# Recurrence heads of a hybrid decoder block: queries and keys scaled up the levels, the next head's projections in eight pieces

## What is computed

```python
qf = jax.nn.silu(q)
log_f = jnp.logaddexp(jnp.log(lb), jnp.log1p(-lb) + jax.nn.log_sigmoid(z))
k = -jnp.expm1(log_f)
def step(state, inp):            # one chunk of 64 tokens
    q_, k_, lf, v_ = inp
    b = jnp.cumsum(lf, axis=2)
    diff = b[:, :, :, None, :] - b[:, :, None, :, :]
    decay = jnp.exp(jnp.where(causal, diff, -jnp.inf))
    scores = jnp.einsum('bhtk,bhsk,bhtsk->bhts', q_, k_, decay)
    o = (jnp.einsum('bhts,bhsv->bhtv', scores, v_)
         + jnp.einsum('bhtk,bhkv->bhtv', q_ * jnp.exp(b), state))
    new_state = (jnp.exp(b_last)[..., None] * state
                 + jnp.einsum('bhsk,bhsv->bhkv', k_ * jnp.exp(b_last[:, :, None, :] - b), v_))
```

## Time and profile before

| | |
|---|---|
| runs (3) | 1618.0 to 1621.55 us, median 1621.48 us |
| profiled execution | 1621.46 us; span of its instructions 1619.6 us |
| PE, share of the span | 90% busy |
| VectorE, ScalarE | 50%, 40% busy |
| this stage | 155.6 to 362.6 us of the span |

### The profile page before, as it was taken

The page is one execution under the profiler, slowest core; times in us unless marked ns, Lnnn a source line. Parts: engine busy times, 40 slices in busy tenths (PEclk is TensorE's granted clock), DMA queues, the critical chain, the costliest instruction groups (busy, mean ns, idle before and its releaser), DMA issues. The chain is left out here.

```text
span 1619.6 us, 19494 instructions
## 1 busy us (share of the span) xinstructions
PE 1464.4 (90%) x7862; PEld 1222.1 (75%) x7862; DVE 805.5 (50%) x971; ACT 644.6 (40%) x760; POOL 108.0 (7%) x86
## 2 busy tenths in 40 slices
PE   6999789869886899979999999999699999995997
PEld 5887667757665688858888888988588888884786
DVE  5410677763332553421222113415489999885654
ACT  5310455421111432211111113133288888885554
POOL 0000000000000000000000000012312222221000
PEclk9999799979999899989999999999599999997999
DMA  6201100004212111122122113721689999994231
GB/s 222 79 1 39 33 14 14 26 4 115 53 26 51 28 41 51 39 61 59 58 69 61 58 58 124 254 92 53 264 322 380 389 385 389 383 370 182 79 110 46
DMA packets 103767, 205.66 MB, mean 127 GB/s; under 512 B 12944, under 2 KB 72976, under 8 KB 90128
## 3 DMA queue, kind: packets, MB, share of 16 engines
q1 hardware_dynamic: 94480, 187.88, 33.1%
q0 software_dynamic: 9216, 16.80, 2.8%
HBM read 188.38 MB, written 28.84 MB: 134 GB/s over the span
## 5 line engine op out<-in xcount | busy, mean ns | idle before, releaser
L1248 DVE TENSOR_TENSOR two_chunk_lo<-two_chunk_raw,two_hi 128x2048 fp32r<-128x2048 f32 x96 | 217.2, 2287 | 21.0 <-ACT two_hi L1244 20.8
L1244 ACT CAST two_hi<-two_chunk_raw 128x2048 fp32r<-128x2048 f32 x96 | 181.2, 1918 | 7.1 <-DMA two_chunk_raw<-w_e 7.1
L220 DVE TENSOR_TENSOR mix_w_lo<-mix_w_raw,mix_w_hi 128x1024 fp32r<-128x1024 f32 (+1 forms) x58 | 67.6, 1170 | 215.3 <-ACT mix_w_hi L216 215.3
L173 PE MATMUL two_banks<-mix_hT_hi,mix_w_hi 128*128 128x512 f32 x256 | 100.5, 393 | 10.0 <-DVE mix_w_lo L220 10.0
L2241 PE MATMUL two_banks<-two_hi,two_xT_hi 128*128 128x512 f32 x256 | 104.0, 406 | 4.2 <-DVE two_xT_lo L1584 4.2
L216 ACT CAST mix_w_hi<-mix_w_raw 128x1024 fp32r<-128x1024 f32 (+1 forms) x58 | 56.9, 986 | 111.6 <-PE two_banks L175 93.2
L2243 PE MATMUL two_banks<-two_hi,two_xT_lo 128*128 128x512 f32 x256 | 101.3, 396 | 0.0
L2242 PE MATMUL two_banks<-two_chunk_lo,two_xT_hi 128*128 128x512 f32 x256 | 101.3, 396 | 0.0
L174 PE MATMUL two_banks<-mix_hT_lo,mix_w_hi 128*128 128x512 f32 x256 | 100.3, 392 | 0.0
L175 PE MATMUL two_banks<-mix_hT_hi,mix_w_lo 128*128 128x512 f32 x256 | 100.3, 392 | 0.0
L173 PE MATMUL gate_gates<-mix_hT_hi,mix_w_hi 128*128 128x512 f32 x192 | 76.5, 398 | 4.5 <-DVE mix_w_lo L220 4.5
(11 more groups left out here) (288 smaller groups left out, 3360.2 us busy)
## 6 DMA issues: line engine op xcount, KB each, us to landing
two_chunk_raw<-w_e SPq DMA_DIRECT2D x102, 1024.0 KB
mix_w_raw<-w_in SPq DMA_DIRECT2D x44, 512.0 KB, 3.8
two_r<-results SPq DMA_DIRECT2D x16, 512.0 KB, 5.0
vals_w_raw<-w_in SPq DMA_DIRECT2D x12, 512.0 KB, 8.6
heads_values<-x SPq DMA_DIRECT2D x8, 512.0 KB, 11.5
reten_swapped<-reten_raw SPq DMA_DIRECT2D x8, 512.0 KB, 5.3
mix_w_raw<-w_b SPq DMA_DIRECT2D x8, 512.0 KB, 4.8
two_x<-x SPq DMA_DIRECT2D x8, 512.0 KB, 6.5
```

The lines of the kernel that those rows point to most:

```text
L173: nc.tensor.matmul(out, sh, mh, start=(k == 0), stop=False)
L220: self.nc.vector.tensor_tensor(self.lo[:, u, 0:kt], self.raw[:, u, 0:kt], self.hi[:, u, 0:kt].bitcast(F32), ALU.subtract).then_inc(self.lo ...
L1244: self.nc.scalar.copy(self.high(n)[:], self.raw(n)[:]).then_inc(self.hi_ok, 1)
L1248: self.nc.vector.tensor_tensor(self.low(n)[:], self.raw(n)[:], self.high(n)[:].bitcast(F32), ALU.subtract).then_inc(self.lo_ok, 1)
```

## The change

The logarithm, the running sum and the exponentials go. ScalarE makes f, the forget gate, and k times its gain directly. `block_totals` multiplies f pairwise up the levels, so that for every block of 1, 2, 4, ... 64 tokens the product of f over it is there. Q starts as q times f and K as k; after the pair of a level, `scale` multiplies, in place, the keys of each lower block by the total of the upper one and the queries of each upper block by the total of the lower one. The levels go from h = 1 up to h = 32. Behind the last, Q and K are what the state terms need, so the former `q_in` and `k_out` go too. Values are read from `values` directly; the GpSimd copy goes. The next head's two projections are cut into eight pieces of 12 matmuls each and put between the pairs; turned keys have two banks of their own, state products use the pair banks and these, and results go into the z sums' banks. Loops over heads are written out.

```diff
+    PAIRED, UP = NL + 1, 2 * NL
+    PIECES = [(half, part) for half in range(2) for part in range(2)]
...
-        ga, gb_, gc = m.sb("sig_z", [P, S]), m.sb("sig_minus_z", [P, S]), m.sb("sig_q", [P, S])
-        q, k, b = m.sb("q", [P, S]), m.sb("k", [P, S]), m.sb("b", [P, S])
-        X = m.sb("scaled", [P, 3, S])
-        q_in, k_out = m.sb("q_in", [P, S]), m.sb("k_out", [P, S])
+        f, q = m.sb("f", [P, S]), m.sb("q", [P, S])
+        Q, K, totals = m.sb("q_scaled", [P, 2, S]), m.sb("k_scaled", [P, 2, S]), m.sb("totals", [P, 2, S])
...
-        kv = m.ps("kv", [P, 4, P])
-        outs = m.ps("outs", [P, 4, HG_DV])
+        turned = [m.ps("turned0", [P, 4, P]), m.ps("turned1", [P, 4, P])]
...
+        kv = [[pairs[:, n].rearrange("p t c -> p (t c)").rearrange("p (t v) -> p t v", v=P) for n in range(2)],
+              [turned[0], turned[1]]]
...
+        def outs(half):
+            return sums[:, 1, half].rearrange("p (t v) -> p t v", v=P)
...
+        def total(i, h):
+            start = S - 2 * S // h
+            return f[:] if h == 1 else totals[:, i % 2, start:start + S // h]
...
-        @block.gpsimd
-        def _(pool):
-            def head(i):
-                if not first(i):
-                    pool.wait_ge(out_ok, 2 * i)
-                nc.gpsimd.tensor_copy(v[:], values[:, :, bass.ds(i * HG_DV, HG_DV)]).then_inc(v_ok, 1)
-            over(pool, HG_HEADS, head)
...
-            def level(i, l):
-                act.wait_ge(sub, 2 * NL * i + 2 * l + 2)
-                nc.scalar.activation(X[:, l % 3, :], X[:, l % 3, :], ACT.Exp).then_inc(expd, 1)
...
+            def gates_z(i):
                 act.wait_ge(projected, 2 * i + 1)
+                nc.scalar.activation(sig_z[:], z_of(i), ACT.Sigmoid).then_inc(sig, 1)
+                nc.scalar.activation(sig_minus_z[:], z_of(i), ACT.Sigmoid, scale=-1.0).then_inc(sig, 1)
+                act.wait_ge(sig, 3 * i + 1)
+                if i:
+                    act.wait_ge(up, UP * (i - 1) + 2)
+                nc.scalar.activation(f[:], sig_z[:], ACT.Identity, bias=lb[:, 1, i:i + 1],
+                                     scale=lb[:, 2, i:i + 1]).then_inc(f_ok, 1)
+                act.wait_ge(sig, 3 * i + 2)
+                nc.scalar.activation(K[:, i % 2], sig_minus_z[:], ACT.Copy, scale=lb[:, 2, i:i + 1]).then_inc(k_ok, 1)
+            def gates_q(i):
                 act.wait_ge(projected, 2 * i + 2)
+                if i:
+                    act.wait_ge(q_ok, i)
+                nc.scalar.activation(sig_q[:], sums[:, 0].rearrange("p a b -> p (a b)"), ACT.Sigmoid).then_inc(sig, 1)
+            gates_z(0)
+            ring.split_hi(act, 1, 0)
+            gates_q(0)
+            ring.split_hi(act, 1, 1)
+            for i in range(HG_HEADS):
+                if i + 1 < HG_HEADS:
+                    gates_z(i + 1)
+                if i + 2 < HG_HEADS:
+                    ring.split_hi(act, i + 2, 0)
+                for half in range(2):
                     act.wait_ge(k_turned, 2 * i + half + 1)
+                    nc.scalar.copy(k_tok[:, 4 * half:4 * half + 4, :], turned[half][:]).then_inc(k_tok_ok, 1)
+                if i + 1 < HG_HEADS:
+                    gates_q(i + 1)
+                if i + 2 < HG_HEADS:
+                    ring.split_hi(act, i + 2, 1)
                 for half in range(2):
                     act.wait_ge(out_ok, 2 * i + half + 1)
+                    nc.scalar.copy(values[:, 4 * half:4 * half + 4, i * HG_DV:(i + 1) * HG_DV],
+                                   outs(half)).then_inc(out_stored, 1)
...
-            def exponents(l):
-                h = LEVELS[l]
-                lower, upper = halves(b[:], h)
-                x_lower, x_upper = halves(X[:, l % 3, :], h)
-                ref = lower[:, :, h - 1:h].to_broadcast([P, S // (2 * h), h])
-                nc.vector.tensor_tensor(x_upper, upper, ref, ALU.subtract).then_inc(sub, 1)
-                nc.vector.tensor_tensor(x_lower, ref, lower, ALU.subtract).then_inc(sub, 1)
...
+            def block_totals(i):
+                dve.wait_ge(f_ok, i + 1)
+                for n in range(NL):
+                    h = 1 << n
+                    if n:
+                        dve.wait_ge(total_ok, NL * i + n)
+                    even, odd = even_odd(total(i, h))
+                    nc.vector.tensor_tensor(total(i, 2 * h), even, odd, ALU.mult).then_inc(total_ok, 1)
+            def queries(i):
+                dve.wait_ge(sig, 3 * i + 3)
+                nc.vector.tensor_tensor(q[:], sums[:, 0].rearrange("p a b -> p (a b)"), sig_q[:], ALU.mult).then_inc(q_ok, 1)
+                dve.wait_ge(q_ok, i + 1)
+                dve.wait_ge(f_ok, i + 1)
+                nc.vector.tensor_tensor(Q[:, i % 2], q[:], f[:], ALU.mult).then_inc(q_scaled, 1)
+            def scale(i, n):
+                h = 1 << (n - 1)
+                of_lower, of_upper = even_odd(total(i, h))
+                dve.wait_ge(paired, PAIRED * i + n + 1)
+                if n == 1:
+                    dve.wait_ge(q_scaled, i + 1)
+                else:
+                    dve.wait_ge(total_ok, NL * i + n - 1)
+                    dve.wait_ge(up, UP * i + 2 * n - 2)
+                lower = halves(K[:, i % 2], h)[0]
+                nc.vector.tensor_tensor(lower, lower, bc(of_upper, 2, h), ALU.mult).then_inc(up, 1)
+                upper = halves(Q[:, i % 2], h)[1]
+                nc.vector.tensor_tensor(upper, upper, bc(of_lower, 2, h), ALU.mult).then_inc(up, 1)
+            def mask(i, n):
+                level = NL - n
+                dve.wait_ge(paired, PAIRED * i + n + 1)
+                if i or n:
+                    dve.wait_ge(masked, PAIRED * i + n)
+                if i and n == 0:
+                    dve.wait_ge(out_ok, 2 * i)
+                nc.vector.tensor_copy(tick[:, level:level + 1], lb[:, 3, 0:1]).then_inc(ticked, 1)
+                nc.vector.copy_predicated(scores[:], bc(masks[:, level, :], 1, TT), pairs[:, n % 2]).then_inc(masked, 1)
+            def states(i, g):
+                dve.wait_ge(kv_ok, 2 * i + g + 1)
+                if g == 0:
+                    dve.wait_ge(total_ok, NL * i + NL)
+                if i and g == 0:
                     dve.wait_ge(out_ok, 2 * i)
                     dve.wait_ge(state_ok, SU * i)
+                for c in range(8 * g, min(8 * g + 8, SU)):
+                    if c:
+                        dve.wait_ge(state_ok, SU * i + c)
+                    nc.vector.scalar_tensor_tensor(out=state[:, c + 1, :], in0=state[:, c, :],
+                                                   scalar=total(i, HG_CHUNK)[:, c:c + 1],
+                                                   in1=kv[g][c % 2][:, (c // 2) % 4, :],
+                                                   op0=ALU.mult, op1=ALU.add).then_inc(state_ok, 1)
+            block_totals(0)
+            ring.split_lo(dve, 1, 0)
+            queries(0)
+            for i in range(HG_HEADS):
+                scale(i, 1)
+                mask(i, 0)
+                mask(i, 1)
+                scale(i, 2)
+                mask(i, 2)
+                if i + 1 < HG_HEADS:
                     ring.split_lo(dve, i + 1, 1)
+                for n in range(3, PAIRED):
+                    scale(i, n)
+                    mask(i, n)
+                if i + 1 < HG_HEADS:
+                    block_totals(i + 1)
+                if i + 2 < HG_HEADS:
+                    ring.split_lo(dve, i + 2, 0)
+                states(i, 0)
+                states(i, 1)
+                if i + 1 < HG_HEADS:
+                    queries(i + 1)
+            def piece(i, u, n):
+                half, part = PIECES[n]
+                if n == 0:
+                    pe.wait_ge(ring.lo_ok, 2 * i + u + 1)
+                    if i and u == 0:
+                        pe.wait_ge(sig, 3 * i - 1)
+                    if i and u:
+                        pe.wait_ge(q_ok, i)
+                    if i >= 2 and u == 0:
+                        pe.wait_ge(out_stored, 2 * (i - 1))
+                cols = slice(half * HALF, (half + 1) * HALF)
+                out = sums[:, 1 - u, half, :]
+                for k in range(4 * part, 4 * part + 4):
+                    wh, wl = ring.hi[:, u, k, :], ring.lo[:, u, k, :]
+                    hh, hl = kept["hT_hi"][:, k, cols], kept["hT_lo"][:, k, cols]
+                    nc.tensor.matmul(out, wh, hh, start=(k == 0), stop=False)
+                    nc.tensor.matmul(out, wh, hl, start=False, stop=False)
+                    mm = nc.tensor.matmul(out, wl, hh, start=False, stop=(k == KT - 1))
+                if n == len(PIECES) - 1:
+                    mm.then_inc(projected, 1)
...
-                pair(0)
-                pair(1)
-                pair(2)
-                pair(3)
-                keys(0)
-                if not at(i, HG_HEADS - 1):
-                    project_z(i + 1)
-                pair(4)
-                keys(1)
-                pair(5)
-                updates(0)
```

(105 more changed lines are left out.)

197 lines of the change are left out of this document (12 added, 185 removed).

## The result

Before, the kernel takes 1620.84 us (median of 4 runs, 1618.0 to 1621.55), changed 1584.61 us (4 runs, 1582.37 to 1584.99): ratio 0.977, 95% interval 0.9757 to 0.9785. It is 36.2 us faster; forecast were 31.3, with 1590.2 us in a range of 1579 to 1603. The profiled execution of the changed kernel took 1584.99 us, its span is 1583.1.

A forecast was written before the change was run, and what follows sets the result against it. The stage was taken as bound by the PE-VectorE handoff. Head 3 starting 32.2 us earlier but giving 1.0 back ends the stage 31.3 us sooner: 1621.46 - 31.3 = 1590.2 us, range 1579 to 1603.

The forecast's parts named there:

- PE's sum and its edges: PE's work per head with eight pieces: 38.5 us, a piece 2.93 us, of which edges add 1.2 us a head.
- VectorE's fit: VectorE's level work fits under a 2.93 us piece: scale 1.30 us (upper bound 3.0), scale and mask 2.1 of 3.9.
- rival 3: Scale costs its upper bound, so PE waits between piece and pair: 13 us more, 1603 us; chance 0.06.
- The turn and head 0: Between heads: no wait in heads 1 and 2; head 0 waits 1.75 and 1.0 us for outputs, lasting 38.3 us.
- The clock: PE's granted clock: 1.00 in heads 1 and 2, falling in head 3 after three fast pairs.
- rival 2: PE runs at 1.2 GHz in the interleaved heads too, 29.6 us a head; at half the time 1634.7 us; chance 0.04.
- rival 1: The clock falls behind head 0's end waits, 6.9 us, and head 3 is slow throughout, 2.5 more: 1599.6 us; chance 0.13.
- Head 3: Without projections between pairs, a closed loop with three fast pairs, the rest slow: 35.6 us, where before had 34.6.
- the tail: End of head 3, keys through updates, outputs and store: 15.3 us at the low clock, 11.1 at 2.4 GHz.
- rival 4: What the stage saves comes back behind it: 1621 us; chance 0.04.

The follow-up runs named there:

- e3_dve2: The changed kernel with two extra multiplications of 512 elements on VectorE in every level of heads 0 to 2, between pair and scale: 1588.95 us.
- e3_dve4: The changed kernel with four extra multiplications of 512 elements on VectorE in every level of heads 0 to 2, between pair and scale: 1612.96 us.
- e1_whole: The changed kernel with the next head's projections whole again, z behind pair 3 and q behind the state products, no early piece: 1626.47 us.
- e4_fill: The changed kernel with five 128x512 multiplications that nobody reads behind each of pairs 1 to 6 of head 3: 1579.96 us.
- e6_fill_reten: The changed kernel with the first retention head's two projections in eight pieces in head 3, whose results go to the pair banks: 1574.68 us.
- e7_late_consts: As e6_fill_reten, but ScalarE and VectorE of the retention stage wait for their constants only where they read them: 1566.83 us.
- e5_no_early: The changed kernel without the early projection piece in head 0: 1584.57 us.
- e8_whole_fill: As e1_whole, with five multiplications that nobody reads behind every pair without a projection behind it, in all four heads: 1602.64 us.

## Why the prediction held, and where it was off

**PE's sum and its edges: right.** A piece 2.94 against 2.93. The head came out at 37.8 instead of 38.5, with the eight keys in one go of 205.85 - 205.06 = 0.79 instead of two times 0.58, updates of 209.75 - 208.76 = 0.99 instead of 1.09, and pairs of 1.08, pair 0 of 0.98. The slots read from the kernel before were a little long for this order.

**VectorE's fit: right.** Scale 1.29 against 1.30 with 3.0 as upper bound; rival 3 has no wait between piece and pair to stand on. e3_dve2 and e3_dve4 bound the room. Totals took 204.93 + 1.45 - 204.22 = 2.16 us against 2.4. Two readings in that paragraph were off without harm. A level has 189.04 - 185.01 = 4.03 us and not 3.9. And pair 2 does not wait for a scale alone: mask 0, which it needs, stands behind scale 1, 2.1 us in all. That fits under 2.94 as well, but it is where e3_dve2 waited first.

**The turn and head 0: right.** No wait in heads 1 and 2; 1.96 and 0.93 at the end of head 0 against 1.75 and 1.0; head 0 is 37.85 long against 38.3.

**The clock: right, in head 0 with luck.** In the interleaved heads it is 1.00 (rival 2). The Trainium skill (TensorE: Matmul & The Clock Gate, section "A second HAM failure mode: psum-queue depth-cycling") tells of a clock that goes up and down where PE is idle for moments between groups while the kernel cycles banks. In heads 1 and 2 PE goes from the projection's banks to others and back with every piece, without an idle moment, and the clock stays up. So the change of banks alone doesn't bring it about; where PE does idle between groups, for 1.4 to 2.2 us in e1_whole, the clock is 0.81 to 0.83.

In head 0 the clock did not fall (rival 1), neither in this execution nor in those of e4_fill and e6_fill_reten. In e7_late_consts, which has the same code as e6_fill_reten in the whole stage, it fell behind the same wait:

```profile
212.22 1.09 PE L773 MATMUL both_sums<-hgrn_state,hgrn_q_scaled 128*64 128x128 f32 x16 [1.96 <-DVE hgrn_state L651]
213.24 1.85 PE L777 MATMUL both_sums<-heads_values,hgrn_scores 64*64 64x128 f32 x16
```

There it cost 0.7 us (218.04 - 212.22 = 5.82 from output(0) to the next pair 0, instead of 217.85 - 212.76 = 5.09), since the clock was back before pair 0; rival 1 had put it at 6.9. So the sum was right to leave this term out, but nothing in its argument told the two outcomes apart.

**Head 3: right but for its tail.** Pair 0 to the first slow pair 300.25 - 293.45 = 6.80 us (6.8 forecast), four more turns 313.75 - 300.25 = 13.50 (13.5 forecast), the tail 326.75 - 313.75 = 13.0 instead of 15.3. The term was mis-sized by 2.3 us. I had left the clock low to the end, while the last two groups of calls took 1.09 each, at 2.4 GHz: 1.5 us. Keys and updates(0) took 1.90 and 1.68 us at the low clock, against 1.3 and 1.2 times 1.98 / 1.15, 2.2 and 2.1: most of the rest.

**The difference, added up.** Stage end 326.75 against 331.3: 0.4 at the start (the stage before ended that much sooner), 0.45 in head 0, 0.7 in each of heads 1 and 2, 2.3 in head 3, together 4.55. From the stage's end to that of the span it is 0.7 us less than before (1256.35 against 1257.03), so nothing is given back (rival 4); 0.7 us is less than that part differs between executions (e5_no_early: 1253.4). 1590.2 - 4.55 - 0.7 = 1584.95, the measured 1584.99.

**What it had not said.** The prediction priced both parts in one sum and so didn't see how little either is worth alone. Its own words on head 3, a closed loop where no projection is put between, hold for every level of e1_whole but the one with the projection, and I did not apply them there. The range was also wider than its chance: by the prediction's own figures rivals 1 and 3 lie inside it too, 0.92 in all, where it says eight in ten.

## What to carry to other kernels

Before two engines' work is interleaved, write both loads for one level side by side: what the interleaving can give is the wait in that level and what the clock loses behind it (7.4 and 6.0 us a head here), and the load of the other engine must fit under one piece, with the handoffs. Two halves of such a change can each be worth nothing or less, so an experiment with one half alone says little of the whole. After every gain look at what the removed work had hidden, at the stage's tail and behind its barrier above all: a wait for data put at the head of a stream, rather than where the data is read, cost 7.9 us once its cover had gone.

## What the runs showed of the hardware that I had not expected

Giving PE work that nobody needs made a kernel faster twice, by 23.8 us (e8_whole_fill) and 4.6 us (e4_fill), since it replaced waits of 1.4 us behind which TensorE had been granted 1.2 GHz. Waits between lone pairs brought the clock down each time: in head 3 of the changed kernel the pair behind a wait of 2.18 us was still at 1.15, the next one, behind a further 1.39, at 1.98, and so it went in head 3 of e1_whole. With pieces of a projection between, it stayed up behind waits of nearly the same length: in e3_dve4 PE waits 1.2 to 2.0 us before most pairs of heads 1 and 2, and all pairs there take 1.10 to 1.15. A single wait came out either way: behind 1.96 us at the end of head 0 all calls took 1.09 in three executions, the second 16 took 1.85 in a fourth (e7_late_consts), and behind 1.95 us in e3_dve2 already the first 16 took 1.98. No run here varied the length of one such wait by itself, so where the border lies stays open.
